# The modulation's weight rows on ScalarE's DMA queue, one engine to round all weights, and a new table that places the expert rows

## What is computed

```python
mod = jax.nn.silu(c) @ w_ada[l] + b_ada[l]
shift1, scale1, gate1, shift2, scale2, gate2 = jnp.split(mod[:, None, :], 6, axis=-1)
h = rms_norm(x, norm1_w[l]) * (1.0 + scale1) + shift1
...
ub = jnp.take(u, eb, axis=0)                      # 128 experts per token
hid = jax.nn.gelu(jnp.einsum('tkd,td->tk', ub, xb), approximate=False) * gb
vb = jnp.take(v, eb, axis=0)
return jnp.einsum('tk,tkd->td', hid, vb)
```

## Time and profile before

| | us |
|---|---|
| median of three runs | 3083.5 (3074.08 to 3090.07) |
| the profiled execution, its own time | 3080.89 |
| its span | 3079.2 |
| busy PE, DVE, POOL, ACT | 2407.3, 1799.2, 1487.6, 801.0 |
| mean granted clock of PE | 0.882 of full |
| moved by DMA | 758.89 MB, 246 GB/s over the span |

### The profile page before, as it was taken

The page is one execution under the profiler, slowest core; times in us unless marked ns, Lnnn a source line. Parts: engine busy times, 40 slices in busy tenths (PEclk is TensorE's granted clock), DMA queues, the critical chain, the costliest instruction groups (busy, mean ns, idle before and its releaser), DMA issues.

```text
span 3079.2 us, 33119 instructions
## 1 busy us (share of the span) xinstructions
PE 2407.3 (78%) x11936; PEld 1694.9 (55%) x11936; DVE 1799.2 (58%) x3817; ACT 801.0 (26%) x1748; POOL 1487.6 (48%) x1239
## 2 busy tenths in 40 slices
PE   7998745456887789979999999899667776667676
PEld 7867745456867675657787866567222222222222
DVE  5444444445664876576765677665765466654444
ACT  2132300000242232343533345333211112121111
POOL 5613222224412331145544455364877777777764
PEclk9958877778858895589999999899999999999998
DMA  5513334344413563478999998597999999999997
GB/s 183 173 53 117 109 129 141 133 138 161 137 35 106 163 229 122 137 265 310 339 331 346 337 342 316 197 351 273 351 345 354 370 348 360 357 351 371 365 349 265
DMA packets 228579, 758.89 MB, mean 246 GB/s; under 512 B 23985, under 2 KB 49601, under 8 KB 227522
## 3 DMA queue, kind: packets, MB, share of 16 engines
q0 software_dynamic: 147456, 536.94, 48.3%
q1 hardware_dynamic: 80962, 219.85, 20.9%
HBM read 751.97 MB, written 4.72 MB: 246 GB/s over the span
## 4 chain that ended last, share of the span: by engine, by line
PE 43%; POOL 21%; DVE 15%; DMA 10%; issue 8%; ACT 2%; another core or an unknown queue 1%; SPq 0%; DVEq 0%; POOLq 0%; ACTq 0%
POOL rings L524 10%; POOL rings L516 10%; PE bank L1266 8%; PE bank L921 8%; PE bank L923 8%; PE bank L922 8%; DMA weights<-in_w_ff 6%; PE bank L1024 3%; DVE weights_split L1296 2%; DMA rings<-in_peer_v,scratch 2%; DVE area L1439 1%; DVE rings L1739 1%; PE bank L1007 1%; DVE weights_split L1299 1%; PE bank L991 1%
## 5 line engine op out<-in xcount | busy, mean ns | idle before, releaser
L1266 PE MATMUL bank<-rings,weight_diagonals 128*128 128x512 f32 x1944 | 957.9, 625 | 293.5 <-DMA rings<-in_peer_v,scratch 225.7
L1266 PEld LDWEIGHTS bank<-rings,weight_diagonals 128*128 128x128 f32 x1944 | 350.1, 196 | 832.5 <-issue 668.1
L1739 DVE CUSTOM_DVE_ANT_0 rings<-rings,token_rows 128x1024 f32<-128x1024 f32 x512 | 617.2, 1223 | 316.4 <-DMA rings<-in_peer_u,scratch 283.4
L524 POOL DMA_INDIRECT rings<-in_peer_v,scratch x512 | 573.7, 1120 | 471.1 <-PE bank L1266 320.6
L516 POOL DMA_INDIRECT rings<-in_peer_u,scratch x512 | 590.8, 1154 | 400.6 <-DVE scratch L1739 247.3
L921 PE MATMUL bank<-h_T_high,weights_split 128*128 128x256 f32 (+1 forms) x1376 | 422.5, 307 | 146.0 <-POOL weights_split L467 106.7
L466 POOL CAST weights_split<-weights 128x1024 fp32r<-128x1024 f32 x86 | 95.4, 1109 | 693.6 <-DMA weights<-in_w_ff 314.2
L1299 DVE TENSOR_TENSOR weights_split<-weights,weights_split 128x1024 fp32r<-128x1024 f32 x242 | 300.0, 1250 | 207.7 <-ACT weights_split L549 161.0
L922 PE MATMUL bank<-h_T_low,weights_split 128*128 128x256 f32 (+1 forms) x1376 | 405.3, 295 | 0.0
L923 PE MATMUL bank<-h_T_high,weights_split 128*128 128x256 f32 (+1 forms) x1376 | 404.5, 294 | 0.0
L877 ACT ACTIVATE weight_diagonals<-ident,scratch 128x128 f32<-128x128 f32 x486 | 190.3, 400 | 767.6 <-PE bank L1266 448.6
(11 more groups left out here) (319 smaller groups left out, 3197.6 us busy)
## 6 DMA issues: line engine op xcount, KB each, us to landing
weights<-in_w_ff SPq DMA_DIRECT2D x128, 512.0 KB
weights<-in_w_in SPq DMA_DIRECT2D x88, 512.0 KB
area<-in_w_ada SPq DMA_DIRECT2D x48, 512.0 KB, 4.7
weights<-in_w_out SPq DMA_DIRECT2D x32, 512.0 KB
weights<-in_w_pq SPq DMA_DIRECT2D x32, 512.0 KB
weights<-in_w_mq SPq DMA_DIRECT2D x16, 512.0 KB
weights<-in_w_mo SPq DMA_DIRECT2D x16, 512.0 KB
rings<-in_peer_u,scratch POOLq DMA_INDIRECT x512
```

The costliest lines, as they stand in the source:

```text
L524: pool.indirect_dma_start(vring[k], None, A["peer_v"], index(n)).then_inc(v_landed[k], 16)
L1266: ins = pe.matmul(bank[half][:], wdiag[:, i % 4, :], vring[d % RV][:, half * COLS:(half + 1) * COLS], start=(r == 0), stop=(r == SLOTS - 1))
L1739: dve.tensor_tensor_reduce(out=uring[k], in0=uring[k], in1=token[:, b % 2, :], scale=1.0, scalar=0.0, op0=ALU.mult, op1=ALU.add, accum_out ...
```

## The change

Three things are changed. The rows of `w_ada` are issued by ACT at the end of its steps of the feed-forward instead of by SP, and DVE's `modulate` moves from the end of its step to the front (two rows in each of steps 0 to 23). ACT copies the high part of every half of both passes (`fed = [0]`, with a first feed of mk ahead of `turned`), and POOL (even halves of pass 0) and DVE only subtract, after waiting for `w_high`. `STAGES` has new times and a count of chunks per stage, and `mark` gives each stage (us - 2.9 x chunks) / 2.76 rows. By that formula "ff" gets 38.8 rows, "in" 17.1, "in2" 13.4, "fox" and "chk" 16.7 each, "wq" 14.8, "gla" 15.9, "swa" 13.0, "out", "mo", "out2" 5.2 each, "mq" 4.9; 211.9 in all. SP's load of FINROW, which waits for `top_done` of row 160, moves from the first chunk of out2 to the first of wq.

```diff
-STAGES = [("mixn", 1, 10), ("in", 12, 70), ("fox", 20, 42), ("chk", 20, 38), ("y", 1, 9), ("out", 4, 23), ("post0", 1, 10),
-          ("memn", 1, 5), ("mq", 4, 23), ("mem", 12, 22), ("memy", 1, 5), ("mo", 4, 23), ("post1", 1, 10), ("ffn", 1, 5),
-          ("ff", 32, 186), ("post2", 1, 10), ("attn", 1, 6), ("in2", 10, 60), ("swa", 20, 28), ("gla", 10, 45), ("mixed", 1, 6),
-          ("out2", 4, 23), ("add", 1, 5), ("peern", 1, 8), ("wq", 8, 53)]
-LENGTH = sum(us for _, _, us in STAGES)
-ROWS_WITHIN = 232
+STAGES = [("mixn", 1, 14, 0), ("in", 12, 82, 12), ("fox", 20, 46, 0), ("chk", 20, 46, 0), ("y", 1, 11, 0), ("out", 4, 26, 4), ("post0", 1, 12, 0),
+          ("memn", 1, 4, 0), ("mq", 4, 25, 4), ("mem", 12, 16, 0), ("memy", 1, 7, 0), ("mo", 4, 26, 4), ("post1", 1, 12, 0), ("ffn", 1, 4, 0),
+          ("ff", 32, 200, 32), ("post2", 1, 12, 0), ("attn", 1, 6, 0), ("in2", 10, 66, 10), ("swa", 20, 36, 0), ("gla", 10, 44, 0), ("mixed", 1, 8, 0),
+          ("out2", 4, 26, 4), ("add", 1, 12, 0), ("peern", 1, 6, 0), ("wq", 8, 64, 8)]
+CHUNK_US, ROW_US = 2.9, 2.76
 def mark(stage, i=0):
     at = 0.0
-    for name, n, us in STAGES:
+    for name, n, us, chunks in STAGES:
+        rows = (us - CHUNK_US * chunks) / ROW_US
         if name == stage:
-            return int((at + us * (i + 1) / n) * ROWS_WITHIN / LENGTH)
-        at += us
+            return int(at + rows * (i + 1) / n)
+        at += rows
...
-                if p == 0 and name in ("f1", "f2"):
-                    for r in range(rows, min(48, 2 * (c - ORD[0, "f1", 0] - 1))):
-                        if r >= 2:
-                            sp.wait_ge(ada_used, r - 1)
-                        sp.dma_start(ada[:, r % 2, :], A["w_ada"][r]).then_inc(ada_landed[r % 2], 16)
-                        rows = r + 1
...
-                if key == (1, "out2", 0):
+                if key == (1, "wq", 0):
                     sp.wait_ge(top_done, 2 * QUARTERS)
...
-                pool.wait_ge(w_landed[w % W_SLOTS], 16 * (w // W_SLOTS + 1))
-                link(pool.tensor_copy(high, raw))
+                pool.wait_ge(w_high, w + 1)
                 pool.tensor_tensor(low, raw, high.bitcast(F32), ALU.subtract).then_inc(w_split_pool, 1)
...
-            fed = [2 * FIRST[1]]
+            fed = [0]
...
+            def modulations(lo, hi):
+                for r in range(lo, hi):
+                    if r >= 2:
+                        act.wait_ge(ada_used, r - 1)
+                    act.dma_start(ada[:, r % 2, :], A["w_ada"][r]).then_inc(ada_landed[r % 2], 16)
...
                         squares(N_MIX, b, X[:, b, :])
+                    feed(ORD[p, "mk", 0])
                     turned(p, N_MEM)
...
                     act.activation(crow, crow, ACT.Silu).then_inc(c_ready, 1)
+                    modulations(0, 2)
...
+                    if p == 0 and t < 23:
+                        modulations(2 * t + 2, 2 * t + 4)
...
-                    if w < 2 * FIRST[1]:
-                        if w % 2 == 0:
-                            continue
-                        dve.wait_ge(w_landed[w % W_SLOTS], 16 * (w // W_SLOTS + 1))
-                        link(dve.tensor_copy(high, raw))
-                    else:
-                        dve.wait_ge(w_high, w - 2 * FIRST[1] + 1)
+                    if w < 2 * FIRST[1] and w % 2 == 0:
+                        continue
+                    dve.wait_ge(w_high, w + 1)
                     dve.tensor_tensor(low, raw, high.bitcast(F32), ALU.subtract).then_inc(w_split, 1)
...
                 for t, (kind, f) in enumerate(FF_ORDER):
+                    if p == 0:
+                        if t == 0:
+                            dve.wait_ge(c_ready, 1)
+                        if t < 24:
+                            modulate(2 * t)
+                            modulate(2 * t + 1)
+                        if t == 24:
+                            modulated()
                     feed(ORD[p, kind, f] + 1)
                     if kind == "f1":
                         hidden_split(p, f)
-                    if p == 0:
-                        if t == 1:
-                            dve.wait_ge(c_ready, 1)
-                        if 1 <= t < 25:
-                            modulate(2 * t - 2)
-                            modulate(2 * t - 1)
-                        if t == 26:
-                            modulated()
```

More of the change, by code:

```diff
@@ L374, in rest @@
                     sp.dma_start(X[:, b, :], A["x"][b]).then_inc(x_landed[b], 16)
-            rows = 0
             for c, (p, name, i) in enumerate(ORDER):
```

## The result

The changed kernel takes 2939.3 us in the median of four runs (2934.3 to 2954.7), the one before 3078.8 in four runs of the same comparison. The ratio is 0.955, 95% interval 0.950 to 0.960. I had predicted 2913 within 2845 to 2990. The profiled execution took 2939.1 us, span 2936.1.

What follows compares the result with a forecast made beforehand. Pass 0's feed-forward was taken as bound by weights behind SP's wait on DVE's modulate, pass 1's by PE, rows alone by DMA. -179 - 4 + 13 = -170 on 3080.9 gives 2911, as median 2913 us; range 2845 to 2990.

Steps and rivals of the forecast that it cites:

- part 3: New marks: 20.1 more rows run alone (+59.3 us), stages of pass 1 change by -46.1; +13 us, bounds -68 and +54.
- Part 1: Pass 0's feed-forward: w_ada rows leave SP's queue, so 24 steps fall to 7.8 us each; -179 us.
- a chain of two steps: Pass 0's feed-forward: modulates, subtraction, PE's odd half, squares, issue, landing, modulates; 14.0 to 17.2 us for two steps.
- ScalarE's wait for modulates: Sign in pass 0's feed-forward: ACT would wait only shortly for modulates; no size in us given.
- The 9.0 us a step: Pass 0's feed-forward: step length if a POOL subtraction blocked DVE in each two-step chain; the whole 28 us later.
- Part 2: ACT rounds all halves: worth sought outside the feed-forward, in PE's waits on split weights; -4 us, bounds -8 to +8.
- all others, +23.0 rows: Pass 1's remaining stages, such as fox and chk: added rows cost DVE's 1.2 us each; +27.6 us.
- in2, out2, wq, -10.2 rows at 1.78: -18.2: These stages of pass 1: 10.2 fewer rows save 1.78 us each; -18.2 us.
- PE-bound at once: Rival, pass 0's feed-forward: landings fit under the tile, step near 6.1 us; 41 us less, 2873; chance 0.16.
- longer loop: Rival, pass 0's feed-forward: lower PE clock, POOL blocking DVE, landings of 7.9; step 10.8 us, 2985; chance 0.16.
- no more than the issue: Rival, pass 0's feed-forward: transfers limit, the move saves only 1.47 us in 23 steps, 34 us; 3058; chance 0.03.
- Slower: Rival, pass 0's feed-forward: ACT's queue closes the loop every step, 15.5 us; with marks at +54, 3134; chance 0.03.

Runs made afterwards that it cites:

- e3: Kernel before plus only the w_ada rows issued by ACT and DVE's modulates in front, old rounding and marks: ratio 0.945, step 8.40 us.
- e7: e1 with ACT issuing the w_ada rows before it waits for the tile in f1 steps of pass 0: ratio 0.938, step 7.26 us.
- e9: e1 with four slots for the w_ada rows instead of two, ACT issuing one step further ahead: ratio 0.932, step 6.64 us.
- e11: e1 with both four w_ada slots and no subtraction on GpSimd: ratio 0.927, step 6.42 us.
- e10: e1 with two slots kept and GpSimd's subtraction left out, VectorE subtracting both halves: ratio 0.941, step 8.13 us.
- e4: Kernel before plus only the rounding on ACT, w_ada rows still in SP's queue, old marks: ratio 0.995, step 14.93 us.
- e1: Changed kernel with the old stage table and marks (232 rows) and FINROW loaded at out2 again: ratio 0.939, step 7.15 us.
- e2: Kernel before with only the new stage table, new mark and FINROW load at wq: ratio 1.013, step 15.78 us.
- e8: Changed kernel with old marks, but rows moved from swa and gla into the feed-forward, total still 232: ratio 0.940.
- e6: Changed kernel with the last four pick steps of block 1 moved to rows 149 to 152, in in2: ratio 0.953, gla 71.4 us.
- e12: e11 with VectorE's modulates behind its subtraction and hidden split, ACT issuing one step later: ratio 0.929, step 6.36 us.

## Why the prediction was right, and where it was not

The total came within 26 us of the forecast, by two errors of opposite sign: pass 0 ended some 8 us earlier than the sum said, and part 3 cost 35 us more.

**Part 1, right in size, its chain wrong.** SP's wait in front of the weights was the loss, as the earlier trace rows said: alone it is worth 160 us (e3) and with the rounding 192. I took 7.8 us a step from a chain of two steps; it is 7.16. That the two come so near is in part luck: moving the issue out of the chain through PE's half tile and ScalarE's squares won nothing (e7), while four slots won 0.5 us a step (e9). The loop that goes round without a pause is that of one slot, with VectorE against GpSimd behind it (e9, e11), and the two chains happen to be of nearly the same length. Its landing is 5.4 us, inside my 4.7 to 7.9. PE's clock stayed up, 0.97, as the earlier trace rows let hope. I had also left a part of the gain unnamed: I wrote of some 10 us a step of waiting, but PE idled 7.8 us a step, and its own work took 7.9 us at clock 0.72 instead of 6.1 at 0.97. One sign of mine did not come true: ScalarE's wait for modulates was to be short, and it is 60.5 us in 19 waits.
DVE's modulates took 1.54 us with GpSimd's subtraction beside them and 1.22 without (e10). By the Trainium skill, "SBUF: State Buffer", section "SBUF: two separate sides", the two engines lock each other out of a shared port pair, and the trace agrees: the 17 modulates that started inside a subtraction of GpSimd ended as if they had begun at its end. The 9.0 us a step that I worked out for a collision in every chain did not come; the measured 7.16 decides.

**Part 2, mis-sized.** I gave it -4 us as a term of its own. It is worth 18 us alone (e4) and 32 on top of part 1 (848.1 against 880.4), all of it in the feed-forward of pass 0 (e4's steps are 18.4 us shorter than before, its other stages together 0.6 us longer; e3's feed-forward is 32.5 us longer than e1's, from the first subtraction to the last). The step that failed is that I looked for its worth outside the feed-forward only, and had put VectorE's 2.84 us copy out of the new chain silently, as if part 1 had removed it. The total was right since my 7.8 us already had no copy in it.

**Part 3, the term that failed.** Predicted +13 us, measured +48, and 40 to 49 by e1 and e2; inside my bounds of -68 and +54. The rows alone (+59 predicted, +63) and the feed-forward (-37, -32) came as priced, and that PE and not DMA bounds the feed-forward is confirmed: 1.62 us a row (31.6 us for the 19.5 rows that left this stretch, and e8), a little under my 1.78. Two steps failed, both behind the feed-forward. The first is "all others, +23.0 rows, at VectorE's 1.2 us". In fox, chk and swa it held: 2.9, 2.9 and 3.6 us more for 4, 3 and 3.5 rows. In gla it did not, +14.3 us for 3 rows, because the top-k steps are tied to row numbers: shifting the marks moved 11 us of VectorE's work from in2 into gla (e6). I had listed the row instructions and left out what `between` hangs on them. The second is "in2, out2, wq, -10.2 rows at 1.78: -18.2". Nothing was saved there: with 4.5 rows and those 11 us of top-k less, the stretch up to swa got 2.3 us longer, and the one behind gla, with one row less, 9.0. The picks don't explain that, as e6 put them back and won 2.5 us. In these stretches PE idled more (4.3 us before and 7.4 after up to swa, 4.6 and 10.9 behind gla) and ran at a lower clock (0.94 and 0.96, before 0.98 and 0.99), and behind gla ScalarE waited for weights to land. Why is open.

**The rivals.** PE-bound at once is what e11 and e12 come near, not the change. The longer loop did not come, nor did "no more than the issue": the pair of issues takes about 1.5 us and the gain was 8.6 us a step. By the Trainium skill, "DMA: Bandwidth & Descriptors", section "Issuing engines are not separate DMA queues", a second issuing engine saves only the time to start transfers; here it also took a wait out of the queue that feeds PE, which is where the gain lay. Slower did not come for the whole, but the marks by themselves are slower (e2).

## What to carry to other kernels

A transfer that must wait for a consumer should not stand in the queue that feeds the main stream; look at what an issuing queue waited for before looking at bandwidth. When work is placed into other stages, price it by the engine that bounds each stage, measured by moving some of it, and not by the transfer time that the stage leaves idle; and move with it, in the sum, everything that is counted by it. A price that held for adding rows to a stage, or for taking them out of one, isn't thereby the price in the next. A step that lands near its measured time does not show that the chain behind it is the right one.

## What the runs showed of the hardware beyond that

The rate of the rows alone differs between chips. On the chip of e1 to e4 the kernel before took 3029.9 us and on that of e12 3031.3, on the others 3073.8 to 3078.8; e1's rows alone ran at 377 GB/s with a DMA share of 0.99 (last line of its fence above), 2.78 us a row, those of e9 at 354 GB/s and 0.95. All five runs on the two faster chips have 375 to 379 GB/s there, all others 351 to 362. The rows alone of e9:

```profile
1930.90:2765.00 834.10, 579.25 (x1243) 211.17 (x1241) 484.93 (x1220) 147.62 (x345) 624.48 (x560) 0.98 0.95 354
```

So times of whole runs are compared here as ratios to runs on the same chip. The PE-bound feed-forward of pass 1 takes 297.0 us on both kinds. And leaving GpSimd's subtraction out, with nothing else changed, made pass 0 slower by 16 us with two slots, but in e11, where it is left out on top of four slots, faster by 16: the same edit has either sign, by what else stands in VectorE's way.
